# Split passes for the recurrent gates and the gate spreads of a one-layer hybrid backbone, with the convolution dealt over two pieces

## The reference, cut to what matters

```
hx = modulate(rms_norm(x, g_mix), sh1, sc1)            # hc likewise from ctx
... x_lru ... = split(hx @ w_in)                       # eight slices of 512
x_conv = centred_depthwise_conv(x_lru, conv_w, conv_b) # four taps, per channel
r = sigmoid(block_diag_linear(z, w_r, b_r))            # z = x_conv or c_conv
i = sigmoid(block_diag_linear(z, w_i, b_i))            # four groups of 128 channels, two directions
log_a = -8 * r * softplus(-lam);  a = exp(log_a)
b = sqrt(-expm1(2 * log_a)) * (i * z)
h = scan(a, b), forwards and backwards, context first
y_lru = (hx_f + hx_b) * gelu(x_lg)
x = x + gt1 * (sum_n sigmoid(hx @ w_gate[n]) * (y_n @ w_branch[n])) @ w_out
x = x + gt2 * swiglu(modulate(rms_norm(x, g_ffn), sh2, sc2))
```

## Time and profile before

| what | value |
|---|---|
| time, median of 3 runs | 1639.59 us (1638.05 to 1640.97) |
| profiled execution, its own time | 1638.07 us |
| its span | 1636.4 us |
| TensorE matmul busy | 1607.0 us, 98% |
| VectorE busy | 1098.0 us, 67% |
| ScalarE busy | 726.4 us, 44% |
| GpSimd busy | 159.6 us, 10% |

### The profile page before, as it was taken

The page is one execution under the profiler, slowest core; times in us unless marked ns, Lnnn a source line. Parts: engine busy times, 40 slices in busy tenths (PEclk is TensorE's granted clock), DMA queues, the critical chain, the costliest instruction groups (busy, mean ns, idle before and its releaser), DMA issues.

```text
span 1636.4 us, 22699 instructions
## 1 busy us (share of the span) xinstructions
PE 1607.0 (98%) x7899; PEld 1322.7 (81%) x7899; DVE 1098.0 (67%) x1263; ACT 726.4 (44%) x812; POOL 159.6 (10%) x296
## 2 busy tenths in 40 slices
PE   6999999999999999999999999999999999999998
PEld 4678798987788888888787888888888888888876
DVE  4333556878888888878795576867755555555577
ACT  5333234468744444444445544443444444434434
POOL 1002111000022122123010010101100000000000
PEclk9999999999999999999999999999999999999999
DMA  9998746645589899899585677878776666666654
GB/s 345 356 357 243 243 146 203 222 144 158 190 298 326 276 308 329 280 342 342 208 294 157 180 237 243 279 233 267 253 254 192 187 190 192 192 192 187 187 169 139
DMA packets 200545, 390.28 MB, mean 238 GB/s; under 512 B 14400, under 2 KB 47408, under 8 KB 199584
## 3 DMA queue, kind: packets, MB, share of 16 engines
q1 hardware_dynamic: 176960, 312.51, 59.4%
q0 software_dynamic: 23312, 76.79, 14.0%
q10 hardware_dynamic: 208, 0.11, 0.0%
HBM read 386.35 MB, written 3.01 MB: 238 GB/s over the span
## 4 chain that ended last, share of the span: by engine, by line
PE 93%; DMA 3%; DVE 1%; ACT 1%; SPq 1%; issue 1%; POOL 0%; DVEq 0%; POOLq 0%; ACTq 0%
PE ps L1414 25%; PE ps L1416 25%; PE ps L1415 25%; PE ps L1386 4%; PE ps L1387 4%; PE ps L1388 4%; DMA BR<-in_w_mod 2%; PE ps L1382 2%; PE ps L1467 1%; DMA MR<-in_w_mod 1%; DVE LO L788 1%; PE ps L1578 0%; PE ps L1565 0%; PE ps L1604 0%; PE ps L1603 0%
## 5 line engine op out<-in xcount | busy, mean ns | idle before, releaser
L788 DVE TENSOR_TENSOR LO<-RAW,HI 128x1024 fp32r<-128x1024 f32 x519 | 632.8, 1223 | 403.8 <-ACT HI L447 402.4
L447 ACT ACTIVATE HI<-RAW 128x1024 fp32r<-128x1024 f32 x519 | 548.5, 1060 | 759.8 <-PE ps L1416 631.3
L1414 PE MATMUL ps<-HI,H 128*128 128x512 f32 x1840 | 721.9, 392 | 0.7 <-DVE LO L788 0.4
L1416 PE MATMUL ps<-HI,H 128*128 128x512 f32 x1840 | 716.4, 389 | 0.0
L1415 PE MATMUL ps<-LO,H 128*128 128x512 f32 x1840 | 716.0, 389 | 0.0
L1414 PEld LDWEIGHTS ps<-HI,H 128*128 128x128 f32 x1840 | 345.4, 188 | 74.7 <-issue 2.2
L1415 PEld LDWEIGHTS ps<-LO,H 128*128 128x128 f32 x1840 | 345.5, 188 | 72.4 <-issue 1.9
L1416 PEld LDWEIGHTS ps<-HI,H 128*128 128x128 f32 x1840 | 345.4, 188 | 72.4
L409 POOL DMA_DIRECT2D BR<-in_w_mod x224 | 120.4, 538 | 766.4 <-DVE BR L900 305.8
L900 DVE SCALAR_TENSOR_TENSOR BR<-BR,SCF 128x512 f32<-128x512 f32 (+1 forms) x210 | 156.8, 747 | 12.6 <-DMA BR<-in_w_mod 10.9
L1386 PE MATMUL ps<-H,HI 128*128 128x256 f32 (+1 forms) x384 | 125.6, 327 | 0.1
(11 more groups left out here) (257 smaller groups left out, 749.9 us busy)
## 6 DMA issues: line engine op xcount, KB each, us to landing
RAW<-in_w_gate SPq DMA_DIRECT2D x128, 512.0 KB, 4.7
BR<-in_w_mod POOLq DMA_DIRECT2D x224, 256.0 KB, 4.6
RAW<-in_w_ffn_gate SPq DMA_DIRECT2D x88, 512.0 KB, 3.7
RAW<-in_w_ffn_up SPq DMA_DIRECT2D x88, 512.0 KB, 3.7
RAW<-in_w_ffn_down SPq DMA_DIRECT2D x88, 512.0 KB, 3.6
RAW<-in_w_in SPq DMA_DIRECT2D x64, 512.0 KB, 5.3
BR<-in_w_mod SPq DMA_DIRECT2D x50, 512.0 KB, 9.4
RAW<-in_w_branch SPq DMA_DIRECT2D x32, 512.0 KB, 5.4
```

The lines of the kernel that those rows point to most:

```text
L447: act.activation(HI[:, j % RING, :], RAW[:, j % RING, :], ACT.Copy).then_inc(hi_done, 1)
L788: tt(LO[:, j % RING, :], RAW[:, j % RING, :], HI[:, j % RING, :], ALU.subtract).then_inc(lo_done, 1)
L1414: mm(o, xh, wh, start=first and t == 0, stop=False, skip_group_check=True)
L1416: i = mm(o, xl, wh, start=False, stop=last and t == 1, skip_group_check=True)
```

## The change

- The recurrent gates: ScalarE makes `GATES_HI`, a high copy of the gate weights of one group, at pieces 53, 55, 56 and 59; GpSimd makes `GATES_LO`. ScalarE makes `ZH` from `Z` at LRU_AT - 2, GpSimd `ZL`. TensorE does each of the four products of a block in the three passes of `rows3`. It waits for `gates_lo` and `conv_lo` in place of `conv`.
- The convolution: first two passes at LRU_AT - 5, last two at LRU_AT - 4, each after everything else of that piece.
- The spreads: ScalarE makes a high copy of each sum, VectorE the low part, TensorE multiplies the ones (fp32r) by each.
- `HS` moves to another place in SBUF, and some semaphores are merged (constants, stores, halves).

```diff
+LRU_SPLIT_AT = (53, 55, 56, 59)
...
+        SUMS_HI = [[H[:, 0, 8 * g + n, :, :].rearrange("p l t -> p (l t)") for n in range(4)] for g in range(2)]
...
+        ZH = BRR[:, 11872:12384]
+        ZL = BRR[:, 11360:11872]
+        GATES = SW[:, 8:24, :].rearrange("p (w d g) n -> p g w d n", w=2, d=2)
+        GATES_LO = BRR[:, 9312:11360].rearrange("p (w d g n) -> p g w d n", w=2, d=2, g=G4)
...
             with pool.Fori(0, EARLY) as g:
                 mod_group(g, MR, 2, "mod_landed", 3 * D)
+            for g in range(G4):
+                pool.wait_ge(s("gates_hi"), g + 1)
+                pool.tensor_tensor(GATES_LO[:, g], GATES[:, g], GATES_HI[:, g], ALU.subtract).then_inc(s("gates_lo"), 1)
+            for g in range(G4):
+                pool.wait_ge(s("conv_hi"), g + 1)
+                if g:
+                    pool.wait_ge(s("lru_mm"), 2 * g)
+                else:
+                    pool.wait_ge(s("sgu_mm"), 1)
+                pool.tensor_tensor(ZL, Z[:, g % 2, :], ZH, ALU.subtract).then_inc(s("conv_lo"), 1)
             pool.wait_ge(s("branches_made"), 1)
...
+                if w in LRU_SPLIT_AT:
+                    g = LRU_SPLIT_AT.index(w)
+                    act.wait_ge(s("small_in"), 16 * 7)
+                    act.wait_ge(used, 8 * 3 + 8 + 4)
+                    act.activation(GATES_HI[:, g], GATES[:, g], ACT.Copy).then_inc(s("gates_hi"), 1)
+                if w + 2 in LRU_AT:
+                    g = LRU_AT.index(w + 2)
+                    act.wait_ge(s("conv"), g + 1)
+                    if g:
+                        act.wait_ge(s("lru_mm"), 2 * g)
+                    else:
+                        act.wait_ge(s("vn"), 2)
+                    act.activation(ZH, Z[:, g % 2, :], ACT.Copy).then_inc(s("conv_hi"), 1)
...
+            def sums_high(g, n, src, groups):
+                act.wait_ge(s("mod_used"), groups * KT + 2)
+                act.activation(SUMS_HI[g][n], src, ACT.Copy).then_inc(s("sums_hi"), 1)
...
-                if w + 3 in LRU_AT:
+                for g in range(G4):
+                    if w not in (LRU_AT[g] - 5, LRU_AT[g] - 4):
+                        continue
...
+                    if w == LRU_AT[g] - 5:
...
+                        taps = (1,)
+                    else:
+                        taps = (2, 3)
-                    for k in range(1, CONV):
+                    for k in taps:
...
-                        pe.wait_ge(s("conv"), g + 1)
+                        pe.wait_ge(s("gates_lo"), g + 1)
+                        pe.wait_ge(s("conv_lo"), g + 1)
...
                         for d in range(2):
-                            mm(ps[:, 4 + 2 * d, :], SW[:, 8 + 4 * d + g, :], Z[:, g % 2, :], start=True, stop=True)
-                            mm(ps[:, 5 + 2 * d, :], SW[:, 16 + 4 * d + g, :], Z[:, g % 2, :], start=True, stop=True)\
+                            rows3(ps[:, 4 + 2 * d, :], GATES_HI[:, g, 0, d, :], GATES_LO[:, g, 0, d, :], ZH, ZL, True, True)
+                            rows3(ps[:, 5 + 2 * d, :], GATES_HI[:, g, 1, d, :], GATES_LO[:, g, 1, d, :], ZH, ZL, True, True)\
                                 .then_inc(s("lru_mm"), 1)
...
+            def spread(g, n):
+                mm(ps[:, 4 + n, :], ONES, SUMS_HI[g][n], start=True, stop=False)
+                return mm(ps[:, 4 + n, :], ONES, SUMS_LO[g][n], start=False, stop=True)
...
-                pe.wait_ge(s("mod_used"), (8 + first + count) * KT + 2)
+                pe.wait_ge(s("sums_lo"), first + count)
...
-                    i = mm(ps[:, 4 + n, :], ONES, ACCB[:, n % 3, :], start=True, stop=True)
+                    i = spread(0, n)
```

More of the change, by code:

```diff
@@ L151, in build @@
         Y = H[:, 0, :, :, :]
+        GATES_HI = Y[:, 8:12, :, :].rearrange("p g l (h n) -> p g l h n", h=2)
         HID = H[:, 0, 0:G4, :, :]
         HIDL = H[:, 0, G4:2 * G4, :, :]
+        SUMS_HI = [[H[:, 0, 8 * g + n, :, :].rearrange("p l t -> p (l t)") for n in range(4)] for g in range(2)]
+        SUMS_LO = [[H[:, 0, 8 * g + 4 + n, :, :].rearrange("p l t -> p (l t)") for n in range(4)] for g in range(2)]
         SCF = sb("SCF", [P, 2, KT])
@@ L185, in build @@
         HD = ATT[:, 6144:7168]
+        with nc.sbuf_tensor("BRR", [P, 12896], F32R) as BRR:
+            pass
         BR = sb("BR", [P, 12896])
@@ L358, in _ @@
                         sp.wait_ge(s("rows_act"), t + 1)
-                    sp.dma_start(out[0, t * P:(t + 1) * P, n * BW:(n + 1) * BW], OTOK[:, n, t, :]).then_inc(s(f"stored{t}"), 16)
-            for t in range(2):
-                sp.wait_ge(s(f"stored{t}"), 64)
+                    sp.dma_start(out[0, t * P:(t + 1) * P, n * BW:(n + 1) * BW], OTOK[:, n, t, :]).then_inc(s("stored"), 16)
+            sp.wait_ge(s("stored"), 128)
         @block.gpsimd
@@ L684, in _ @@
                     high((OUT0 + 8 * n) // 4, j)
+                    if w < 3:
+                        sums_high(0, w, ACCB[:, w, :], 11)
+                    if w == 24:
+                        sums_high(0, 3, ACCB[:, 0, :], 12)
                     if w == 5:
@@ L753, in _ @@
                 high(PRE0 // 4, w)
+                if w < 4:
+                    sums_high(1, w, ACCG[:, w, :], 16)
                 if w == 5:
@@ L1068, in straight @@
                         split_low("lru_hi", g + 1, Y[:, 8 + g, 1, :], HS, Y[:, 8 + g, 0, :], "lru_lo")
-                if w + 3 in LRU_AT:
-                    g = LRU_AT.index(w + 3)
+                for g in range(G4):
+                    if w not in (LRU_AT[g] - 5, LRU_AT[g] - 4):
+                        continue
                     z = Z[:, g % 2, :].rearrange("p (s t) -> p s t", s=2)
[L1073 to L1078, removed]
-                    for k in range(1, CONV):
+                    if w == LRU_AT[g] - 5:
+                        dve.wait_ge(s("win_read"), 2)
+                        if g == 0:
+                            dve.wait_ge(s("pooled"), 1)
+                        if g >= 2:
+                            dve.wait_ge(s("lru_w"), 2 * (g - 1))
+                        own.did(ts(z, LP[:, g, :, 0:T], PB[:, PB_CW + g:PB_CW + g + 1], PB[:, PB_CB + g:PB_CB + g + 1], ALU.mult, ALU.add))
+                        taps = (1,)
+                    else:
+                        taps = (2, 3)
+                    for k in taps:
                         own.wait()
@@ L1147, in a2, with sums_low @@
                 stt(A2[:, :], MC2[:, KT:2 * KT], 1.0, PA[:, PA_GFFN:PA_GFFN + KT], ALU.add, ALU.mult).then_inc(s("a2"), 1)
+            def sums_low(g, n, src):
+                split_low("sums_hi", 4 * g + n + 1, SUMS_LO[g][n], src, SUMS_HI[g][n], "sums_lo")
             def gate1_row(n):
@@ L1174, in _ @@
                         merged_low(3)
+                    if 8 * n + j in (2, 3, 4):
+                        sums_low(0, 8 * n + j - 2, ACCB[:, 8 * n + j - 2, :])
+                    if 8 * n + j == 25:
+                        sums_low(0, 3, ACCB[:, 0, :])
                     if 8 * n + j in (8, 9, 10):
@@ L1189, in last_scaled @@
                 if t == 0:
-                    dve.wait_ge(s("out_half"), 1)
+                    dve.wait_ge(s("half_done"), 1)
                 else:
@@ L1325, in _ @@
                     hidden_low(FC - 2)
+                if w in (2, 4, 5, 7):
+                    n = (2, 4, 5, 7).index(w)
+                    sums_low(1, n, ACCG[:, n, :])
                 if w in (11, 13):
@@ L1338, in _ @@
                 if w == 21:
-                    dve.memset(ST[:, 3:4], EPS).then_inc(s("eps_set"), 1)
-                    dve.memset(ST[:, 7:8], EPS).then_inc(s("eps_set"), 1)
+                    own.did(dve.memset(ST[:, 3:4], EPS))
+                    own.did(dve.memset(ST[:, 7:8], EPS))
                 if w == 25:
@@ L1351, in last_rows @@
                 if t == 0:
-                    dve.wait_ge(s("last_half"), 1)
+                    dve.wait_ge(s("half_done"), 2)
                 else:
@@ L1361, in last_rows @@
                     dve.wait_ge(s("sqf"), 6)
-                    dve.wait_ge(s("eps_set"), 2)
+                    own.wait()
                     for u in range(2):
@@ L1798, in _ @@
                 if q == 0:
-                    i.then_inc(s("out_half"), 1)
+                    i.then_inc(s("half_done"), 1)
             h2_turn(0)
@@ L1853, in _ @@
             gate_pieces(FC - 1, PRE0)
-            pe.wait_ge(s("mod_used"), 16 * KT + 2)
+            pe.wait_ge(s("sums_lo"), 8)
             pe.wait_ge(s("down_read"), 4 * (FC - 1))
@@ L1858, in _ @@
                 for n in (2 * half, 2 * half + 1):
-                    i = mm(ps[:, 4 + n, :], ONES, ACCG[:, n, :], start=True, stop=True)
+                    i = spread(1, n)
                 i.then_inc(s("gate2_spread"), 1)
```

19 lines of the change are left out of this document (9 added, 10 removed).

## The result

The changed kernel takes 1641.82 us (median of 20 runs, 1640.33 to 1644.33), the kernel before 1638.99 (20 runs, 1637.31 to 1641.00): a ratio of 1.002 with a 95% interval of 1.0013 to 1.0026, or +2.8 us. Forecast were 1637.1, in a range of 1633.4 to 1641.4: wrong in sign. The ratio and its interval are estimated from all the runs and need not be the quotient of the two medians. The profiled execution has a span of 1639.2 us against 1636.4, so its rows tell of the same 2.8.

What follows compares the result with a forecast made beforehand. TensorE, busy 98% of the span, was taken as the bound. Blocks -2.84, spreads -3.26 and chain waits +3.6 gave -2.5 us, so 1637.1 us from a median of 1639.59, range 1633.4 to 1641.4.

Steps and rivals of the forecast that it cites:

- Blocks and spreads: TensorE's four recurrent blocks and eight gate-spread matmuls as split passes: gains of 2.84 and 3.26 us, 6.10 together.
- Splitting the spread's sums at 0: Output projection: added ScalarE copies and VectorE subtractions fit idle time, cost 0; without that cover at most 3 us.
- Gate weights: "Cost 0 as a wait": GpSimd's four subtractions from pieces 53 to 59: TensorE needs the first result 46 us later, so cost 0.
- Conv input split at 0: ScalarE copies Z two pieces early, GpSimd subtracts; over 8 us are available, TensorE will not wait for `conv_lo`: cost 0.
- The convolution moved, 3.6 us: Convolution passes enter the VectorE-ScalarE chain; TensorE waits at pieces 85, 87 and 94 to 97, 3.6 us with signalling.
- the `ZH` copy in ScalarE's row: Copies in both chain turns, 0.6 us each, held free because ScalarE waits for L1066 right behind.
- The 0.1 to 0.15 us of signalling a wait: Addition at each wait for the moved convolution, taking their sum from 3.3 to 3.6 us.
- Nothing behind piece 97: Stage's end: waits were forecast only at pieces 85, 87 and 94 to 97, with no term for later pieces.
- GpSimd holds VectorE: Rival: GpSimd passes hold VectorE at piece 55 and in the chain, costing 4.1 us; 1641.2 us, chance 0.24.
- h: Time each GpSimd pass holds VectorE in the rival: from 0 to 3 us, taken as 1.5.
- The waits do not come: Rival: TensorE waits for nothing in the block stage, the whole 6.1 us gain stays; 1633.5 us, chance 0.22.
- The change does not shorten TensorE: Rival: split passes in the blocks run slower, say 0.28 us, and blocks give nothing; 1638.6, chance 0.08 including something else.

Runs made afterwards that it cites:

- spreads_only: Changed kernel with the recurrent part of the kernel before; only the gate spreads are in two passes: 1635.87 us, ratio 0.9981 to the kernel before.
- weights_later: Changed kernel with the gate-weight copies and GpSimd's four subtractions at pieces 58, 60, 61, 62 in place of 53, 55, 56, 59: 1639.65 us, ratio 1.0002.
- merge_first: Changed kernel with the first merge at piece 100 in place of 101 on VectorE: 1640.48 us, ratio 1.001 to the kernel before.
- no_gpsimd: Changed kernel without its eight GpSimd passes, high parts standing in for low ones: 1637.29 us, ratio 0.999 to the kernel before.
- conv_late: Changed kernel with the convolution whole again at LRU_AT - 3 and the `ZH` copy at LRU_AT - 1, GpSimd's passes kept: 1638.32 us, ratio 1.0002.
- both_out: Changed kernel without GpSimd's passes (low parts left out), convolution whole at LRU_AT - 3, `ZH` copy at LRU_AT - 1: 1636.60 us, ratio 0.9986.
- conv_move_only: Kernel before with only the convolution moved to LRU_AT - 5 and - 4: 1641.23 us, ratio 1.0015.
- gpsimd_only: Kernel before with only eight unused GpSimd subtractions of 128x512 added at the change's places: 1642.21 us, ratio 1.0018.

## Why the prediction was wrong, step by step

*Blocks and spreads.* Right. 2.6 us against 2.84, since a pass is 0.232 apart here and not 0.227; the spreads 3.2 against 3.26, and 3.05 by the medians when timed alone.

*Splitting the spread's sums at 0.* Right: `spreads_only` has no wait for it.

*Gate weights: "Cost 0 as a wait".* This step failed. The argument was that TensorE needs the result 46 us later. That is true, and TensorE never waits for `gates_lo`. But the cost of a GpSimd pass lies in whom it holds while it runs. Two VectorE passes up to the `LO` of piece 55 grew by 0.77 and 0.94 (299.25, 303.70), 1.7 us; the load waited for in front of them adds 0.49, and the rest is that VectorE was already 0.2 us later at this place. The `LO` is 2.44 us later, TensorE itself was 0.2 ahead, the cover was 0.37: 2.3 are left, 2.17 stand as the wait and 2.4 are lost with the restart. Without GpSimd's passes there, 0.2 to 0.8 are lost in place of 2.6, and `weights_later` shows it from the other side.

*Conv input split at 0.* It failed in the same way. `conv_lo` is never waited for, but the passes at 376.60 and 400.86 hold the last scan and L1097 by 0.84 and 1.10, both in the chain between VectorE and ScalarE that ends in L1066's successor. With GpSimd's passes out the losses at pieces 80 to 98 fall from 4.9 to 2.9: 2.0 us.

*The convolution moved, 3.6 us.* The places are right (pieces 85, 87, 94 to 97), the size was 4.9 against 3.6 (whose first wait, 402.4 against 402.1, is 0.3 and stands as 0.4), and the account does not hold. Of the 4.9 us the GpSimd passes make 2.0, the move alone 0.9 (2.9 to 2.0), and 2.0 come with neither. The move was charged with 3.6 alone; that the sum came near is in part luck, since what was left out fills the gap. The 2.0 fit the chain itself: a turn of 22.7 us against TensorE's new one of 21.8. I had that pair of numbers and used it for a rival only; I also held the `ZH` copy in ScalarE's row to be free, which was not tested apart. The 0.1 to 0.15 us of signalling a wait was 0.2 to 0.3. By the traces the move costs 0.9 us over these pieces without GpSimd, 1.0 on the kernel before (and there 1.3 at piece 100) and 3.0 with GpSimd: a price of a step in a chain isn't one number, it depends on what cover the others have left.

*Nothing behind piece 97.* A step left out. The lag goes on to VectorE's read for the first merge (L1144, at 453.10). It ends at 454.32, TensorE's piece 100 goes on at 454.41, and 1.3 us are lost there. The profile names no releaser for this wait; `merge_first` shows it, by taking it away. The same 1.3 us are lost in `no_gpsimd`, `conv_late`, `both_out` and `conv_move_only`, and in neither the kernel before, `spreads_only` nor `gpsimd_only`.

Together: -5.8 + 2.6 + 4.9 + 1.3 is +3.0; TensorE was 0.2 us ahead before piece 53, and the waits between 660 and 800, which scatter, add 0.1. That makes +2.9 against a measured +2.8. The prediction had -6.1 + 3.6: its terms for the gate weights, for the split of Z and for what lies behind piece 97 were 0, and they were 2.6, 2.0 and 1.3.

*The rivals.* "GpSimd holds VectorE" is what happened, with 1641.2 against 1641.8, slower than before. The closeness is luck in part. The rival took three passes held at 1.5 each for 4.1 us; h is 0.8 to 1.1, and four passes are held on the path (two up to piece 55, two in the chain). It had no term for the 1.3 at piece 100. A GpSimd pass takes 1.32 us where it begins ahead of VectorE's and 1.4 to 1.9 elsewhere beside it; the estimate from the Trainium skill ("GPSIMD Engine Reference", "Performance versus the Vector engine") was 1.1. The Trainium skill's rule in "SBUF — State Buffer", "Who interferes with whom", by which a VectorE instruction with two SBUF inputs and a GpSimd instruction that reads SBUF exclude each other whole, is what the stretched rows look like; this trace agrees (0.77 to 1.11 us of growth), and I had it in hand and gave its rival 0.24. "The waits do not come" fell: no kernel with the convolution in the order of the change was without them. "The change does not shorten TensorE" fell with 2.78 us a block.

## What to carry to other kernels

Ask of work given to an idle engine not only when its result is needed but beside whom it runs: here each GpSimd pass of 128x512 on a busy VectorE took about 1 us of VectorE's time, and the same passes a few pieces later were nearly free for TensorE. When TensorE gets faster, compare its new turn with the turn of the chain that feeds it before adding the gain; where the chain is longer, first take out of it what only happens to stand there (a gate's sigmoid, a merge behind a tail). And follow a lag to its last reader, past the last place where it was first seen.

## What was not expected of the hardware

- The holding is the same for several kinds of work on VectorE with two SBUF operands: subtractions, scalar-tensor-tensor passes and scans all grew by 0.8 to 1.1 us, also where they wrote other buffers than GpSimd read. At 333.64 the GpSimd pass (1.30 us) ran beside two VectorE passes that take one operand from PSUM, and those did not grow (1.29 us for both). At 354.74 VectorE's L833 had begun first and kept its 1.23 us; the GpSimd pass took 1.82.
- 2.9 us of idle time on TensorE were followed by some 3 us at passes 0.43 us apart (granted clock 0.66 over 450 to 455), which cost some 2 us more than the wait. Waits of 2.2 us at piece 55 of `gpsimd_only` and of 2.4 in `merge_first` were followed by the lower clock too (0.68 and 0.66 over 305 to 310), while 2.2 in the changed kernel and 2.4 in `conv_late` were not (1.00). So the length of the wait alone does not tell the two apart, and what does is not shown.
